# Stick-breaking attention with its scores kept in PSUM, in five steps a head instead of eight

## What is computed

```python
z = jnp.einsum("bhqe,bhke->bhqk", qb, k) * SCALE
past = kpos[None, :] < qpos[:, None]
log_1m = jnp.where(past, jax.nn.log_sigmoid(-z), 0.0)
suffix = lax.cumsum(log_1m, axis=3, reverse=True) - log_1m
a = jnp.where(past, jnp.exp(jax.nn.log_sigmoid(z) + suffix), 0.0)
return jnp.einsum("bhqk,bhke->bhqe", a, v)
```

## Time and profile before

| | us |
|---|---|
| median of three runs | 3968.79 |
| lowest, highest | 3958.39, 3971.53 |
| the profiled execution, its own time | 3969.82 |
| its span in the trace | 3968.0 |

### The profile page before, as it was taken

One profiled execution on the slowest core, in us unless ns is written; L12 is line 12 of the kernel. 1 busy time (PEld: TensorE's weight loads), 2 busy tenths in 40 slices (PEclk: granted clock), 3 DMA queues, 4 the chain that ended last, 5 costly groups with the idle time before them and its releaser, 6 DMA issues.

```text
span 3968.0 us, 46039 instructions
## 1 busy us (share of the span) xinstructions
PE 3618.2 (91%) x18162; PEld 2883.1 (73%) x18162; DVE 1647.3 (42%) x2793; ACT 1018.2 (26%) x2100; POOL 2025.2 (51%) x1216
## 2 busy tenths in 40 slices
PE   7798777888889999989899899999999998999999
PEld 5766555676667988767777686887668776777887
DVE  6734443334684322375355412331272454214330
ACT  2134435422210211121244311221121344212210
POOL 4444124564446898854433255665544332455655
PEclk9989778898899999999999999999999999999999
DMA  6623112332464443332211122332222111232222
GB/s 225 228 83 104 51 42 73 119 91 66 157 224 137 136 151 123 122 123 75 70 53 54 43 90 75 96 96 89 108 69 75 64 49 42 73 92 78 92 88 98
DMA packets 109864, 389.25 MB, mean 98 GB/s; under 512 B 12057, under 2 KB 16537, under 8 KB 108242
## 3 DMA queue, kind: packets, MB, share of 16 engines
q1 hardware_dynamic: 89280, 315.10, 24.6%
q10 hardware_dynamic: 20370, 71.20, 5.3%
HBM read 379.93 MB, written 6.32 MB: 97 GB/s over the span
## 4 chain that ended last, share of the span: by engine, by line
PE 66%; DVE 8%; ACT 2%; issue 1%; POOL 1%; DMA 1%; DVEq 0%; ACTq 0%; SPq 0%
PE ps L305 18%; PE ps L306 18%; PE ps L307 18%; PE ps L1333 2%; PE ps L1345 1%; PE ps L395 1%; PE ps L397 1%; PE ps L396 1%; PE ps L900 1%; DVE ada L1797 1%; DVE junk L1797 1%; DVE small_d L1390 1%; PE ps L1313 1%; POOL wlo L2343 1%; DVE ps L942 1%
## 5 line engine op out<-in xcount | busy, mean ns | idle before, releaser
L2341 POOL CAST whi<-raw 128x1024 fp32r<-128x1024 f32 (+1 forms) x606 | 619.2, 1022 | 1881.7 <-DMA raw<-in_w 1881.4
L2343 POOL TENSOR_TENSOR wlo<-raw,whi 128x1024 fp32r<-128x1024 f32 (+1 forms) x606 | 1417.8, 2340 | 48.5
L305 PE MATMUL ps<-hhi,whi 128*128 128x512 f32 x2056 | 854.5, 416 | 127.4 <-DVE hlo L951 22.8
L306 PE MATMUL ps<-hlo,whi 128*128 128x512 f32 x2056 | 828.3, 403 | 0.0
L307 PE MATMUL ps<-hhi,wlo 128*128 128x512 f32 x2056 | 827.2, 402 | 0.0
L305 PEld LDWEIGHTS ps<-hhi,whi 128*128 128x128 f32 x2056 | 395.5, 192 | 258.8 <-issue 46.2
L306 PEld LDWEIGHTS ps<-hlo,whi 128*128 128x128 f32 x2056 | 397.2, 193 | 94.9 <-issue 6.7
L307 PEld LDWEIGHTS ps<-hhi,wlo 128*128 128x128 f32 x2056 | 395.9, 193 | 96.7
L305 PE MATMUL ps<-chi,whi 128*128 128x256 f32 x864 | 264.9, 307 | 22.1 <-DVE cD L624 9.1
L306 PE MATMUL ps<-clo,whi 128*128 128x256 f32 x864 | 253.0, 293 | 0.0
L307 PE MATMUL ps<-chi,wlo 128*128 128x256 f32 x864 | 252.3, 292 | 0.0
(11 more groups left out here) (369 smaller groups left out, 6478.5 us busy)
## 6 DMA issues: line engine op xcount, KB each, us to landing
raw<-in_w SPq DMA_DIRECT2D x574, 512.0 KB, 3.5
ada<-in_ada ACTq DMA_DIRECT2D x96, 512.0 KB, 3.7
raw<-in_w SPq DMA_DIRECT2D x16, 384.0 KB, 3.2
att_toe<-toe_dram ACTq DMA_DIRECT2D x12, 256.0 KB, 3.2
raw<-in_w SPq DMA_DIRECT2D x16, 192.0 KB, 2.3
x<-in_x SPq DMA_DIRECT2D x4, 512.0 KB, 9.1
cond<-in_cc ACTq DMA_DIRECT2D x2, 1024.0 KB, 4.9
kc_dram<-kc ACTq DMA_DIRECT2D x2, 1024.0 KB, 4.9
```

The lines of the kernel that those rows point to most:

```text
L305: nc.tensor.matmul(o, whi[:, buf, c], hi[:, k, 0:n], start=(k == 0), stop=False)
L306: nc.tensor.matmul(o, whi[:, buf, c], lo[:, k, 0:n], start=False, stop=False)
L2341: nc.gpsimd.tensor_copy(whi[:, buf, 0:c], raw[:, buf, 0:c]).then_inc(slab_hi, 1)
L2343: nc.gpsimd.tensor_tensor(wlo[:, buf, 0:c], raw[:, buf, 0:c], whi[:, buf, 0:c].bitcast(F32), ALU.subtract).then_inc(slab_split, 1)
```

## The change

- The scale is applied when the query projection of these heads is copied out of PSUM (tiles 4 and 5), not when the scores are copied.
- A head's four score tiles stay in three PSUM banks: blocks 1 and 3 share bank 2, block 2 has bank 3, block 0 bank 4. ACT reads them there for Abs (one instruction for each bank), DVE for the softplus, and ACT for the final Exp. The copy to SBUF is gone, and `stick_e` too: the softplus steps are made in place in a buffer for the whole head.
- The mask of -1e30 for the diagonal pieces is added by PE, as a matmul of the identity with the mask into the same bank ahead of the scores. The 0/1 mask on the softplus is gone, since softplus of -1e30 is 0.
- The suffix sums are accumulated by PE with negative weights on top of the scores, so the subtraction on DVE is gone, and so is its second mask.
- A head has five steps: scores with Abs and Exp (0), Ln and the softplus on DVE (1), suffix sums of blocks 3, 1, 2 with two Exps (2), suffix sum of block 0 with its Exp (3), values (4). The next head's scores wait until all three Exps of this head have read the banks. The part has 21 steps, not 33. The outputs accumulate in bank 5.
- The masks are two, in another place in SBUF that the softmax heads' bias tiles use before it. ACT therefore waits for the last softmax head before it issues their DMA, and PE waits for the DMA ahead of the first scores.

```diff
-                    nc.scalar.activation(self.dst(m), self.out(m), ACT.Copy).then_inc(self.free(m), 1)
+                    nc.scalar.activation(self.dst(m), self.out(m), ACT.Copy, scale=self.scale(m)).then_inc(self.free(m), 1)
...
-                self.steps = 8 * len(heads) + 1
+            PARTS = ((2, 512), (3, 256), (4, 512))
+            BANK = {1: (2, 0), 3: (2, 384), 2: (3, 0), 0: (4, 0)}
+            FLAT = {1: 0, 3: 384, 2: 512, 0: 768}
+
+            def __init__(self, heads, sp, a, masks, clear=()):
+                self.heads, self.sp, self.a, self.masks, self.clear = heads, sp, a, masks, clear
+                self.steps = 5 * len(heads) + 1
...
+            def suffix(self, j):
+
+                bank, o = self.BANK[j]
+                for i in range(j, 4):
+                    mm = nc.tensor.matmul(pb(bank, T - P * i, o + (i - j) * P),
+                                          self.masks[:, 1, :] if i == j else spread(MINUS_COL), self.flat(self.sp, i),
+                                          start=False, stop=(i == 3), skip_group_check=True)
+                return mm
+
+            def tensor(self, pe, i):
+                if i == 0:
                     for c in self.clear:
                         pe.wait_ge(*c())
+                    pe.wait_ge(tri_loaded, 16)
+                h, step = divmod(i, 5)
                 if h == len(self.heads):
                     return
                 hd = self.heads[h]
...
+                if step == 0:
+                    if h:
+                        pe.wait_ge(self.w, self.w0 + 3 * h)
+                    for j in (1, 3, 2, 0):
+                        bank, o = self.BANK[j]
+                        k = hd["k"][:, j * P:(j + 1) * P]
+                        nc.tensor.matmul(pb(bank, P, o), ident, self.masks[:, 0, :], start=(j != 3), stop=False,
+                                         skip_group_check=True)
+                        mm = nc.tensor.matmul(pb(bank, P, o), k, hd["q"][:, j * P:(j + 1) * P], start=False, stop=True,
+                                              skip_group_check=True)
+                        if j < 3:
+                            mm = nc.tensor.matmul(pb(bank, T - P * (j + 1), o + P), k, hd["q"][:, (j + 1) * P:T],
+                                                  start=False, stop=True, skip_group_check=True)
+                        if j != 1:
+                            mm.then_inc(self.s, 1)
+                if step == 2:
+                    pe.wait_ge(self.p, self.p0 + 3 * h + 2)
+                    self.suffix(3)
+                    self.suffix(1).then_inc(self.su, 1)
+                    self.suffix(2).then_inc(self.su, 1)
+                if step == 3:
+                    pe.wait_ge(self.p, self.p0 + 3 * h + 3)
+                    self.suffix(0).then_inc(self.su, 1)
+                if step == 4:
+                    pe.wait_ge(self.w, self.w0 + 3 * h + 3)
+                    if h >= 2:
+                        pe.wait_ge(self.ev, self.ev0 + h - 1)
+                    for j in range(4):
+                        mm = nc.tensor.matmul(self.out(h)[:, j * P:T], hd["v"](j), self.flat(self.a, j),
+                                              start=(j == 0), stop=(j == 3), skip_group_check=True)
+                    mm.then_inc(self.pv, 1)
+
+            def scalar(self, act, i):
+                if i == 0:
+                    act.wait_ge(*self.clear[0]())
                     act.dma_start(self.masks[:, :, :], tri_in).then_inc(tri_loaded, 16)
+                h, step = divmod(i, 5)
                 if h == len(self.heads):
                     return
+                e0 = self.e0 + 9 * h
+                if step == 0:
+                    for p in range(3):
+                        act.wait_ge(self.s, self.s0 + 3 * h + p + 1)
+                        nc.scalar.activation(self.part(self.sp, p), self.psum(p), ACT.Abs).then_inc(self.e, 1)
+                    for p in range(3):
+                        act.wait_ge(self.e, e0 + p + 1)
+                        sp = self.part(self.sp, p)
+                        nc.scalar.activation(sp, sp, ACT.Exp, scale=-1.0).then_inc(self.e, 1)
+                if step == 1:
+                    for p in range(3):
+                        act.wait_ge(self.e, e0 + 3 + p + 1)
+                        sp = self.part(self.sp, p)
+                        nc.scalar.activation(sp, sp, ACT.Ln, bias=cst[:, ONE_COL:ONE_COL + 1]).then_inc(self.e, 1)
+                if step in (2, 3):
+                    for p in ((0, 1), (2,))[step - 2]:
+                        if h:
+                            act.wait_ge(self.pv, self.pv0 + h)
+                        act.wait_ge(self.su, self.su0 + 3 * h + p + 1)
+                        nc.scalar.activation(self.part(self.a, p), self.psum(p), ACT.Exp).then_inc(self.w, 1)
+
+            def vector(self, dve, i):
+                h, step = divmod(i, 5)
+                if step == 0 and h:
                     dve.wait_ge(self.pv, self.pv0 + h)
                     nc.vector.tensor_copy(self.heads[h - 1]["y"], self.out(h - 1)).then_inc(self.ev, 1)
+                if step == 1:
+                    for p in range(3):
+                        sp = self.part(self.sp, p)
+                        dve.wait_ge(self.e, self.e0 + 9 * h + 6 + p + 1)
+                        nc.vector.scalar_tensor_tensor(sp, self.psum(p), 0.0, sp, ALU.max, ALU.add).then_inc(self.p, 1)
 
...
-        project = Gemm("in_qk", 15, KT, hhi, hlo, T, CopyOut(lambda m: qk_at[m][:, :], T, share=False), ready=norm_mix.ready)
+        project = Gemm("in_qk", 15, KT, hhi, hlo, T, CopyOut(lambda m: qk_at[m][:, :], T, share=False,
+                                                             scale=lambda m: SCALE if m in (4, 5) else 1.0),
+                       ready=norm_mix.ready)
...
-                              zone("stick_z", [P, 1280], 150), zone("stick_sp", [P, 1280], 155),
-                              zone("stick_masks", [P, 3, P], 162), zone("stick_e", [P, T], 160),
-                              clear=[softmax.finished])
+                              zone("stick_sp", [P, 1280], 150), zone("stick_a", [P, 1280], 155),
+                              zone("stick_masks", [P, 2, P], 160), clear=[softmax.finished])
...
-    tri = np.stack([(a < b).astype(np.float32), np.where(a < b, 0.0, NEG).astype(np.float32),
-                    (a >= b).astype(np.float32)], 1)
+    tri = np.stack([np.where(a < b, 0.0, NEG), np.where(a >= b, -1.0, 0.0)], 1).astype(np.float32)
```

More of the change, by code:

```diff
@@ L64 @@
 IDENT, SWAP, BLOCK = 0, P, 2 * P
-EPS_COL, EPS_SMALL, ONE_COL, R1024, R256, R128 = range(3 * P, 3 * P + 6)
+EPS_COL, EPS_SMALL, ONE_COL, R1024, R256, MINUS_COL = range(3 * P, 3 * P + 6)
 N_CST = 3 * P + 6
@@ L1138, in finished, with flat, psum, part @@
             def finished(self):
                 return self.ev, self.ev0 + len(self.heads)
-            def span(self, j):
-                o = sum(T - P * i for i in range(j))
-                return o, o + T - P * j
+            def flat(self, buf, j):
+                return buf[:, self.FLAT[j]:self.FLAT[j] + T - P * j]
+            def psum(self, p):
+                bank, n = self.PARTS[p]
+                return pb(bank, n)
+            def part(self, buf, p):
+                o = (0, 512, 768)[p]
+                return buf[:, o:o + self.PARTS[p][1]]
@@ L1145, in out @@
             def out(self, h):
                 r = self.heads[h]["row"]
-                return ps[r:r + HD, 4 * 512:5 * 512]
-            def values(self, pe, h, j):
-                pe.wait_ge(self.ex, self.ex0 + 4 * h + j + 1)
-                if j == 0 and h >= 2:
-                    pe.wait_ge(self.ev, self.ev0 + h - 1)
-                o0, o1 = self.span(j)
-                mm = nc.tensor.matmul(self.out(h)[:, j * P:T], self.heads[h]["v"](j), self.z[:, o0:o1],
-                                      start=(j == 0), stop=(j == 3), skip_group_check=True)
-                if j == 3:
-                    mm.then_inc(self.pv, 1)
@@ L1178, in tensor @@
-                j -= 4
-                if j == 0:
-                    if h == 0:
-                        pe.wait_ge(tri_loaded, 16)
-                    pe.wait_ge(self.v, self.v0 + 16 * h + 8)
-                if j < 2:
-                    pe.wait_ge(self.cp, self.cp0 + 4 * h + j + 3)
-                else:
-                    pe.wait_ge(self.v, self.v0 + 16 * h + 8 + 2 * (j - 2) + 1)
-                for i in range(j, 4):
-                    o0, o1 = self.span(i)
-                    n = T - P * i
-                    mm = nc.tensor.matmul(pb(2 + j % 2, n, (i - j) * P),
-                                          self.masks[:, 2, :] if i == j else spread(ONE_COL),
-                                          self.sp[:, o0:o1], start=(i == j), stop=(i == 3), skip_group_check=True)
```

101 lines of the change are left out of this document (12 added, 89 removed).

## The result

| | before | changed |
|---|---|---|
| median of the runs on this chip, us | 3970.16 (4 runs) | 3924.88 (4 runs) |
| the profiled execution, its own time | 3969.82 | 3924.05 |
| its span in the trace | 3968.0 | 3922.2 |
| mean granted clock of the span | 0.948 | 0.956 |

The ratio of the changed kernel to the one before is 0.9893, 95% interval 0.9871 to 0.9915: faster by 45 us on medians, 42 by the ratio. The forecast was 3931 with a range of 3914 to 3955.

A forecast was written before the change was run, and what follows sets the result against it. The stick-breaking stretch was taken as bound by PE, losing some 11 us a head to the chain from scores to softplus. Terms -54 (stick), +18 (softmax), -2 (behind) gave -38: median 3931 us, range 3914 to 3955.

The forecast's parts named there:

- The own case: Whole kernel: the author's main expectation, 3931 us with a range of 3918 to 3944, chance 0.60.
- The stick stretch: Time while the stick-breaking heads run: 128 us against 182, minus 54.
- The stick work itself: PE's scores, suffix sums and values in four stick heads, 40 us, plus 5 for masks and split scores: 45.
- The term for the masks: Stick heads on PE: 16 mask matmuls and 12 more scores cost 1.2 us a head, 5 in all.
- The start: First stick scores: 4.3 us idle for the masks' DMA and 3.7 for scores at half speed, 8 us; bounds 0 and 12.
- The waits: Stick heads on PE: 5 us ahead of suffix sums over four heads, 4 us for epilogues queued behind DVE's Ln wait.
- the 4 us of other half-speed work: Stick heads: PE work at half speed apart from the first scores, 4 us.
- The softmax stretch: Softmax heads: moved filler priced at 25 us, shorter waits minus 5, better clock minus 2: plus 18; bounds -5 and +28.
- Behind the stretch: Group norm after the stick heads: the last head's copy has 5 us of filler behind it on PE, gaining 2 us.
- That the gaps take the moved work: Softmax heads: PE's idle gaps absorb the moved filler, growth 5 us instead of 18; 3918 us, chance 0.10.
- The blocked filler: Stick heads: filler tiles wait for banks whose epilogues stand behind DVE's Ln wait, 20 us more; 3951 us, chance 0.17.
- the slower case: Stick heads: one bank set and filler not covering the chain, stretch 186 us; time near 3996, chance 0.05.

The follow-up runs named there:

- the last two runs on scores: Changed kernel with masks loaded early and one score matmul per block: 3920.0 us, stick stretch 109.1; the same with a head's mask matmuls first: 3915.7 us, 104.4.

## Why the prediction was right, and where its terms were off

**The bound and the direction held.** PE's idle time and its clock were what the change could win, and most of it was won: of 45.3 idle us in the stick stretch 6.2 are left. The own case was 3931 with 3918 to 3944, and the runs gave 3924.9.

**The stick stretch: forecast 128, measured 118.6.** Tiles, 21 at 2.85 us, are 59.9 of it as forecast. The stick work itself was forecast at 45 and is 44.2, but by two errors against each other. At full clock a head's suffix sums take 4.2 us (forecast 4.7), values 2.3 (2.7), scores with masks 4.5 (2.7 + 1.2 = 3.9). The term for the masks was mis-sized: 2.2 us a head instead of 1.2. The forecast had 0.32 to 0.36 for a short matmul from rows in which like follows like; between two matmuls of the other row count it is 0.42, and the last two runs on scores show 0.19 for each change.

**The start: forecast 8, measured 10.3.** The wait of 3.99 us was met (forecast 4.3), the first scores at half speed too (8.3 us instead of 4.5). The half speed lasted until 625, though, which takes 2.5 us more from the next tiles. The experiment with early masks took away 9.4 in all. So this term was 2.3 too small, for the half speed that outlasted the first scores.

**The waits: forecast 5 + 4, measured 1.9 + 0.3.** This is the largest error of the stretch. Ahead of the suffix sums PE waits in two heads for 0.95 us, in the others not at all, against 0.5 or 2 in each. No tile waits more than 0.3 us for an epilogue. I had named that as a rival (3951) and left 4 us for it. The softplus took the 0.69 us that it was priced at, but the 1.78 which the prediction sets against it was a mean over collisions with GpSimd and not the price of two sources in SBUF. The run with Ln for each bank shows that this rival was near: 16 loads more in that place bring it back, with 16 us of such waits, and 23 us in all. With no such waits the 4 us of other half-speed work did not come either. From 128: -6.8 for the waits, -4 for that work, +2.3 at the start and -0.8 of stick work give 118.7, against 118.6 measured.

**The softmax stretch: forecast +18, measured +22.6.** PE's busy time grew by 17.2 us, where I had priced the moved work at 25 and better clock at -2. The waits were to shrink by 5; the one for the normalised probabilities shrank by 3.3, from 29.5 us to 26.2. But a wait came in that I had not looked for, at the context branch's spatial gate (line 1691):

```profile
PE ps L1022 <- DVE att_p L1096: 26.2, 14, 3.3
...
PE ps L1691 <- issue: 7.1, 1, 7.1
```

In the kernel before the same instruction (its line 1704) waits 0.9 us. The weave now puts the gate's first matmul right behind the norm that it needs: in the trace the last two instructions of that norm on DVE start at 412.98 and take 1.00 us together, and PE's first matmul starts at 414.08 after 7.12 idle us. The wait follows the filler's placing and nothing else: the kernel before with the filler placed as after has 7.1 us there, the changed kernel with the filler placed as before has 0.9. Its 6.2 us more are about the 5.5 us by which PE's idle time grew; the other waits sum to 0.8 less. So two terms were off against each other: the moved work cost 6 us less than priced, the waits 10 more. That moving that one step would give them back was not tried.

**Behind the stretch: forecast -2, measured 0.** The stick copy did come earlier: it ends 2.5 us before PE's last tile does, where it was 0.9 before. But the norm does not start by it. ACT's first square (line 910, at 726.67) stands behind a gate epilogue of the filler (line 836), and PE's first matmul of the norm waits 1.10 us for DVE's last epilogue (line 862) in both kernels. The term rested on a wait for the copy that no row shows.

**The sum.** Forecast -54 + 18 - 2 = -38; measured by the traces -64.5 + 22.6, or -41.8 before rounding, and -45 by the medians. The stick stretch gave 10 us more than forecast, the softmax stretch took 5 more and the tail 2. That the total came within 4 us by the traces is in part luck: the errors had opposite signs. By causes, from the stretches: grouping the Ln -12.4 (tried in the old shape), the rest of the new shape at the old placing of the filler -23.4, the filler's move -6.0. By the ratios the same steps are about -23, -14 and -5 us, so the first two are firm in sign and rough size, and the last has its sign from the stretches alone. The middle one was not divided further: what the gone copies, DVE steps and mask operations gave, each by itself, is not shown. The last has its sign from the change it comes with: the same move costs 12.3 us in the kernel before.

**The rivals.** That the gaps take the moved work is out: the softmax stretch grew by 22.6, not 5. The blocked filler and the slower case did not occur. Ln for each bank produced the first, in the place that the prediction gave it. A slower kernel came of the filler's move in the old shape, by a chain that the filler no longer covers; that one set of banks can make the changed kernel slower was not produced.

## What to carry to other kernels

- On engines that work in one order, an operation's price is what queues behind it: the same 16 table loads cost nothing in a slack place and 17.6 us ahead of epilogues that free PE's banks. Ask of each block who stands behind it, not only who waits for its result.
- A small DMA that becomes the first thing PE waits for can cost more than its wait: 4.0 us of waiting were 9.4 us of the stretch here, with the work at half speed behind it. Give it a buffer of its own and issue it early.
- Where small matmuls with different row counts alternate, put like with like; and when a part loses steps, look at what the weave moves with it, since that alone was worth -6 us here and +12 in the kernel before.

## What the runs showed of the hardware that was not expected

- The change between matmuls of 128 and of 64 rows, fp32, at full clock: eight matmuls in alternation take 4.50 us, the same eight with one change take 3.34. Six changes fewer save 1.16 us, 0.19 each.
- After 3.99 idle us PE ran 12.7 us at a granted clock of 0.52 although it was busy without a gap. Without that idle time the whole stretch ran at 1.00.
- Sixteen table loads of 1283 ns, switching between Ln and Exp four times in a row in each head, left PE's stretch unchanged to 0.1 us, and the activations between them take 0.20 us each, 0.01 or 0.02 us behind the load.
- A softplus step of 512 columns on DVE takes 0.69 us, whether both sources are in SBUF or one in PSUM. The means of 1784 and 959 ns come from single steps of 2.0 to 2.8 us with both sources in SBUF, all beside GpSimd's subtraction; beside the same instruction a 256-column step with one source in PSUM kept its 0.42 us.
